# Partition sums of the first modulation as one-column products on TensorE, with the last two pieces of sc1 multiplied there too

## What is computed

```python
mod = (silu(c) @ w_ada + b_ada)            # 1024 x 6144 weights
sh1, sc1, g1, sh2, sc2, g2 = jnp.split(mod, 6, axis=-1)
h = rms_norm(x, norm1_g) * (1.0 + sc1) + sh1
proj = h @ w_in                            # q, k, v and pool part u
x = x + g1 * (concat[attention(q, k, v), pooling(u)] @ w_o)
h2 = rms_norm(x, norm2_g) * (1.0 + sc2) + sh2
x = x + g2 * (relu(h2 @ w_mlp_in) ** 2 @ w_mlp_out)
```

## Time and profile before

| what | us |
|---|---|
| median of 3 runs | 965.35 |
| lowest and highest of them | 964.99, 967.53 |
| the profiled execution, its own time | 964.76 |
| its span, first to last instruction | 963.0 |
| PE busy in the span | 923.1 (96%) |
| DVE busy | 656.4 (68%) |
| ACT busy | 491.4 (51%) |
| POOL busy | 348.6 (36%) |

### The profile page before, as it was taken

The page is one execution under the profiler, slowest core; times in us unless marked ns, Lnnn a source line. Parts: engine busy times, 40 slices in busy tenths (PEclk is TensorE's granted clock), DMA queues, the critical chain, the costliest instruction groups (busy, mean ns, idle before and its releaser), DMA issues.

```text
span 963.0 us, 12639 instructions
## 1 busy us (share of the span) xinstructions
PE 923.1 (96%) x4411; PEld 762.8 (79%) x4411; DVE 656.4 (68%) x1000; ACT 491.4 (51%) x874; POOL 348.6 (36%) x342
## 2 busy tenths in 40 slices
PE   1899999998999999999999999999999999999998
PEld 1787788886778888788888788888888888888887
DVE  6976887878554587665566544535687666789896
ACT  1756677778465564645544455454343544333331
POOL 8041211116232443988788877851000000000000
PEclk9999999999999999999999999999999999999999
DMA  9852432214222240765456534548998837997772
GB/s 357 323 170 74 131 110 88 80 54 155 87 88 88 88 153 22 232 203 177 164 168 203 176 132 134 173 143 274 331 354 292 280 98 235 312 323 233 237 248 105
DMA packets 92271, 175.54 MB, mean 182 GB/s; under 512 B 9320, under 2 KB 26288, under 8 KB 92208
## 3 DMA queue, kind: packets, MB, share of 16 engines
q1 hardware_dynamic: 92096, 174.70, 54.0%
q10 hardware_dynamic: 112, 0.04, 0.0%
HBM read 136.95 MB, written 37.75 MB: 181 GB/s over the span
## 4 chain that ended last, share of the span: by engine, by line
PE 84%; DVE 7%; ACT 5%; issue 2%; DMA 1%; SPq 1%; POOL 0%; DVEq 0%; ACTq 0%
PE psum L1965 26%; PE psum L1967 26%; PE psum L1966 25%; PE psum L1961 3%; DMA slots<-in_w_ada 1%; ACT probs L777 1%; PE psum L2041 1%; ACT qT L796 1%; DVE squares L1162 1%; PE psum L2091 1%; PE psum L2022 1%; PE psum L2020 1%; PE psum L2019 1%; ACT probs L785 1%; PE psum L2064 1%
## 5 line engine op out<-in xcount | busy, mean ns | idle before, releaser
L1072 ACT CAST down_operands<-down_raw 128x1024 fp32r<-128x1024 f32 x96 | 100.9, 1054 | 152.5 <-PE psum L1967 57.6
L1965 PE MATMUL psum<-down_operands 128*128 128x512 f32 x448 | 174.3, 389 | 0.0
L1966 PE MATMUL psum<-down_operands 128*128 128x512 f32 x448 | 174.3, 389 | 0.0
L1967 PE MATMUL psum<-down_operands 128*128 128x512 f32 x448 | 174.3, 389 | 0.0
L1701 DVE TENSOR_TENSOR down_operands<-down_raw,down_operands 128x1024 fp32r<-128x1024 f32 x93 | 112.4, 1220 | 16.3 <-ACT down_operands L1072 15.4
L1965 PE MATMUL psum<-h2T,w_operands 128*128 128x512 f32 x272 | 107.4, 395 | 1.9 <-DVE act_quads_a L1645 1.3
L1967 PE MATMUL psum<-h2T,w_operands 128*128 128x512 f32 x272 | 106.0, 390 | 0.0
L1966 PE MATMUL psum<-h2T,w_operands 128*128 128x512 f32 x272 | 105.9, 389 | 0.0
L1917 POOL TENSOR_TENSOR w_operands<-raw,w_operands 128x512 fp32r<-128x512 f32 x56 | 83.1, 1485 | 42.2 <-ACT w_operands L1024 42.2
L1966 PEld LDWEIGHTS psum<-down_operands 128*128 128x128 f32 x448 | 84.1, 188 | 17.6
L1965 PEld LDWEIGHTS psum<-down_operands 128*128 128x128 f32 x448 | 84.1, 188 | 17.5
(11 more groups left out here) (249 smaller groups left out, 1965.5 us busy)
## 6 DMA issues: line engine op xcount, KB each, us to landing
down_raw<-in_w_mlp_out SPq DMA_DIRECT2D x160, 256.0 KB, 4.5
down_raw<-act_scratch SPq DMA_DIRECT2D x112, 256.0 KB, 3.4
raw<-in_w_ada SPq DMA_DIRECT2D x32, 512.0 KB, 4.5
raw<-in_w_mlp_in SPq DMA_DIRECT2D x32, 512.0 KB, 4.8
act_scratch<-act_quads_a SPq DMA_DIRECT2D x64, 256.0 KB, 2.3
act_scratch<-act_quads_b SPq DMA_DIRECT2D x48, 256.0 KB, 3.5
slots<-in_w_ada SPq DMA_DIRECT2D x8, 512.0 KB, 10.5
xh<-in_x SPq DMA_DIRECT2D x8, 512.0 KB, 5.8
```

The source lines that it names most:

```text
L1072: nc.scalar.copy(o[:, 0, :, :], r[:, 0:2, :]).then_inc(op2_hi, 1)
L1965: mm(o, wh, ah, start=first, stop=False, skip_group_check=adds)
L1966: mm(o, wh, al, start=False, stop=False, skip_group_check=adds)
L1967: return mm(o, wl, ah, start=False, stop=last, skip_group_check=adds)
```

## The change

Transposes and free-axis sums are replaced with products of one column. For each 128x128 block n of an accumulator, `column_sum` makes the block the stationary operand and a column of ones the moving one, so that the sum over partitions lands as one PSUM column (bank `at + n // 4`, column `n % 4`). For the last two pieces of sc1 (numbers 6 and 7) DVE does nothing more: the piece itself is the stationary operand, and silu[:, k] the moving column, so that multiplication and sum over partitions happen in one product, accumulated in the same PSUM columns. On PE the sh1 sums are 8 such products; for sc1 there are 8 on piece 6, 8 on `acc_sc` and 8 on piece 7, in that order, and after piece 7's fourth and eighth the two halves are signalled. `keep_clock(6, 2)` goes away. On DVE the copy of `cols` moves to just behind the last sh1 piece, the finish of sh1 becomes one addition of 128x8, and `scale_1` becomes two small instructions. The buffer of piece 6 is free once its products are done (`sc1_used`), that of piece 7 once the second half is signalled. SP, ACT and POOL keep their orders.

```diff
@@ -231,6 +231,7 @@
         EARLY_USE = EARLY // WIDE + 1
         MLP_USE = EARLY_USE + (len(stream) - 4 - EARLY) // RING
         WO_POOL, WO_DVE = (0, 5, 6), (1, 2, 3, 4, 7)
+        SC1_DVE = KD - 2
         JOB_LOADS = (4, 4, 4, 3, 4, 4, 1, 0)
         adaln_jobs = ("sh2", "sc2", "g1", "g2")
         mod_of = {"sh1": SH1, "sc1": SC1, "g1": G1, "sh2": SH2, "sc2": SC2, "g2": G2}
@@ -266,6 +267,7 @@
         g1_in = sem("g1_in")
         mod_turned = sem("mod_turned")
         sc1_turned = sem("sc1_turned")
+        sc1_used = sem("sc1_used")
         mod_taken = sem("mod_taken")
 
         a1_ready = sem("a1_ready")
@@ -472,7 +474,12 @@
             kind, k = stream[before]
             if kind in ("sh1", "sc1"):
 
-                eng.wait_ge(mod_summed, k + 1 + (KD if kind == "sc1" else 0) + (kind == "sc1" and k == KD - 1))
+                if kind == "sc1" and k == SC1_DVE:
+                    eng.wait_ge(sc1_used, 1)
+                elif kind == "sc1" and k == KD - 1:
+                    eng.wait_ge(sc1_turned, 2)
+                else:
+                    eng.wait_ge(mod_summed, k + 1 + (KD if kind == "sc1" else 0))
             elif kind in adaln_jobs:
                 eng.wait_ge(job_summed, KD * adaln_jobs.index(kind) + k + 1)
             elif kind == "x":
@@ -1188,40 +1195,35 @@
                 own_d.wait()
                 v.tensor_scalar(a1_, a3, -1.0, float(np.pi / 2), ALU.mult, ALU.add).then_inc(angles_ready, 1)
 
-            for n in range(2 * KD):
+            for n in range(KD + SC1_DVE):
                 if n >= 1:
                     dve.wait_ge(mod_summed, n)
                 if n < KD:
                     add_piece(acc[:, :], ("sh1", n), n, mod_summed)
-                elif n < 2 * KD - 1:
+                else:
                     add_piece(acc_sc, ("sc1", n - KD), n - KD, mod_summed)
-                else:
-                    a = landed(dve, ("sc1", KD - 1))
-                    for h in range(2):
-                        cut = slice(512 * h, 512 * h + 512)
-                        v.scalar_tensor_tensor(out=acc_sc[:, cut], in0=a[:, cut], scalar=silu[:, KD - 1:KD],
-                                               in1=acc_sc[:, cut], op0=ALU.mult, op1=ALU.add).then_inc(mod_summed, 1)
                 if n == 4:
                     dve.wait_ge(rows_in, 16 * 4)
                     v.tensor_copy(rows[64:72, :], posi[64:72, :]).then_inc(posf_ready, 1)
-                if n == KD + 2:
+                if n == KD - 1:
 
                     dve.wait_ge(rows_turned, 1)
                     v.tensor_copy(cols[:, :], psum[:, 4, 0:72]).then_inc(cols_ready, 1)
-                if n == 2 * KD - 4:
+                if n == KD + 4:
 
                     dve.wait_ge(cols_ready, 1)
                     dve.wait_ge(mod_turned, 1)
-                    v.tensor_reduce(b1, banks(0).rearrange("p (k n) -> p k n", n=P), AX_X, ALU.add).then_inc(mod_taken, 1)
+                    v.tensor_tensor(b1.rearrange("p (h k) -> p h k", h=2), psum[:, 0:2, 0:4],
+                                    cols[:, 8 * SH1:8 * SH1 + 8].rearrange("p (h k) -> p h k", h=2),
+                                    ALU.add).then_inc(mod_taken, 1)
+
+            def scale_1(h):
+
+                c4 = slice(4 * h, 4 * h + 4)
+                if h == 0:
                     dve.wait_ge(mod_taken, 1)
-                    own_d.step(v.tensor_tensor(b1, b1, cols[:, 8 * SH1:8 * SH1 + 8], ALU.add))
-            def scale_1(h):
-
-                c4 = slice(4 * h, 4 * h + 4)
                 dve.wait_ge(sc1_turned, h + 1)
-                own_d.step(v.tensor_reduce(a1[:, c4], bank(2 + h).rearrange("p (k n) -> p k n", n=P), AX_X, ALU.add))
-                own_d.wait()
-                own_d.step(v.tensor_tensor(a1[:, c4], a1[:, c4],
+                own_d.step(v.tensor_tensor(a1[:, c4], psum[:, 2 + h, 0:4],
                                            cols[:, 8 * SC1 + 4 * h:8 * SC1 + 4 * h + 4], ALU.add))
                 own_d.wait()
                 v.scalar_tensor_tensor(out=a1[:, c4], in0=a1[:, c4], scalar=1.0, in1=cols[:, 48 + 4 * h:52 + 4 * h],
@@ -2098,17 +2100,32 @@
             pe.wait_ge(posf_ready, 1)
             tr(psum[:, 4, 0:72], rows[0:72, :], 72).then_inc(rows_turned, 1)
 
+            def column_sum(at, n, a, by, first, last):
+
+                to = psum[:, at + n // 4, n % 4:n % 4 + 1]
+                return mm(to, a[:, n * P:(n + 1) * P], by, start=first and n % 4 == 0, stop=last, skip_group_check=True)
+
             pe.wait_ge(mod_summed, KD)
-            turn_sums(banks(0), acc).then_inc(mod_turned, 1)
+            for n in range(KD):
+                ins = column_sum(0, n, acc, ones[:, 0:1], True, True)
+            ins.then_inc(mod_turned, 1)
             pe.wait_ge(mod_summed, 2 * KD - 5)
             keep_clock(8, 2)
             turn_x(0)
             pe.wait_ge(cols_ready, 1)
             turn_x(1)
-            keep_clock(6, 2)
+            a = landed(pe, ("sc1", SC1_DVE))
+            for n in range(KD):
+                ins = column_sum(2, n, a, silu[:, SC1_DVE:SC1_DVE + 1], True, False)
+            ins.then_inc(sc1_used, 1)
+            pe.wait_ge(mod_summed, KD + SC1_DVE)
+            for n in range(KD):
+                column_sum(2, n, acc_sc, ones[:, 0:1], False, False)
+            a = landed(pe, ("sc1", KD - 1))
             for h in range(2):
-                pe.wait_ge(mod_summed, 2 * KD + h)
-                turn_sums(bank(2 + h), acc_sc[:, 512 * h:512 * h + 512]).then_inc(sc1_turned, 1)
+                for n in range(4 * h, 4 * h + 4):
+                    ins = column_sum(2, n, a, silu[:, KD - 1:KD], False, True)
+                ins.then_inc(sc1_turned, 1)
             pe.wait_ge(mod_taken, 1)
             keep_clock(14, 0)
 
```

More of the change, by code:

```diff
@@ L1206, in _ @@
                     v.tensor_copy(rows[64:72, :], posi[64:72, :]).then_inc(posf_ready, 1)
-                if n == KD + 2:
+                if n == KD - 1:
                     dve.wait_ge(rows_turned, 1)
                     v.tensor_copy(cols[:, :], psum[:, 4, 0:72]).then_inc(cols_ready, 1)
-                if n == 2 * KD - 4:
+                if n == KD + 4:
                     dve.wait_ge(cols_ready, 1)
                     dve.wait_ge(mod_turned, 1)
-                    v.tensor_reduce(b1, banks(0).rearrange("p (k n) -> p k n", n=P), AX_X, ALU.add).then_inc(mod_taken, 1)
-                    dve.wait_ge(mod_taken, 1)
-                    own_d.step(v.tensor_tensor(b1, b1, cols[:, 8 * SH1:8 * SH1 + 8], ALU.add))
+                    v.tensor_tensor(b1.rearrange("p (h k) -> p h k", h=2), psum[:, 0:2, 0:4],
+                                    cols[:, 8 * SH1:8 * SH1 + 8].rearrange("p (h k) -> p h k", h=2),
+                                    ALU.add).then_inc(mod_taken, 1)
             def scale_1(h):
                 c4 = slice(4 * h, 4 * h + 4)
+                if h == 0:
+                    dve.wait_ge(mod_taken, 1)
                 dve.wait_ge(sc1_turned, h + 1)
-                own_d.step(v.tensor_reduce(a1[:, c4], bank(2 + h).rearrange("p (k n) -> p k n", n=P), AX_X, ALU.add))
-                own_d.wait()
-                own_d.step(v.tensor_tensor(a1[:, c4], a1[:, c4],
+                own_d.step(v.tensor_tensor(a1[:, c4], psum[:, 2 + h, 0:4],
                                            cols[:, 8 * SC1 + 4 * h:8 * SC1 + 4 * h + 4], ALU.add))
```

## The result

| | before | after |
|---|---|---|
| median of 20 runs, us | 965.41 | 969.38 |
| lowest and highest | 964.77, 967.53 | 965.51, 975.00 |
| profiled execution | 964.76 | 973.25 |
| its span | 963.0 | 971.5 |

The changed kernel takes 1.0043 times the time of before, 95% interval 1.0030 to 1.0056: **4.2 us slower**. The forecast was 965.8 with a range to 969.2. What is new beside the median is the spread: before, 20 executions lie within 2.8 us, after within 9.5. The lowest of after is 0.7 above the lowest of before, close to the forecast sum.

A forecast was written before the change was run, and what follows sets the result against it. DVE was taken to bound the kernel from 30.47 to 49 us, with PE setting the end behind. A signal 1.90 us later less 1.45 us spared gave +0.45 on 965.35: 965.8 us, range 963.6 to 969.2.

The forecast's parts named there:

- What bounds the kernel: DVE bounds from the first sc1 half's signal (30.47 us) until 49 us; behind that PE sets the end.
- A record at 0.112 us: Each one-column weight load and product on PE costs 0.112 us, as with 128 columns; 0.21 at the slow clock.
- the handover: From the fortieth load to DVE's start: 0.11, a product of 0.17 (0.275 less 0.107 of streaming), and 0.04; 0.32 us.
- Sum +0.45: First sc1 signal +1.90 us later, DVE spared 1.45 us of free-axis sums behind it; net +0.45 us, chance 0.62.
- The step that failed: PE reaches the sc1 columns at 27.68 us, behind the x transposes, and runs 40 records at 0.112 us each.
- a rival at 0.18: PE's clock falls early in the column products, 26 of 40 records slow: +3.7 us, 969.1 us; chance 0.18.
- With all records slow: All column records at the slow clock, with 28 slow filler records behind: w_in at 44.0 us, +6.5, 971.8 us.
- The small edits: sh1 products, the filler behind the columns and later SP loads, each covered by waiting time or slack, cost nothing.
- None of this counts: DVE's savings ahead of the signal (pieces 6 and 7, sh1 sum, cols copy) add nothing, as PE is late next.
- `keep_clock(14, 0)` level, at no cost: Its 28 records behind the last column end near 36.2 us, when project_u(0) can start; no cost.
- PE's slack: 48 w_in products from 35.76 us would end at 46.8, but the last begins at 48.56; some 1.8 us.
- SP and the buffers: The load waiting for piece 7's buffer goes out at 33.3 us, not 30.4; even 2.9 us later it is in time.

The follow-up runs named there:

- a_root: Changed kernel with GpSimd's roots for x tiles 0 and 1 moved ahead of the last pooling band (early roots): 968.12 us, ratio 1.0021.
- b_root: Kernel before with GpSimd's roots for x moved ahead of the last pooling band: 964.55 us, ratio 0.9990.
- probe_columns: Kernel before with 48 one-column products of the identity matrix put between keep_clock(14, 0) and project_u(0): 979.93 us in one execution.
- a_again: Changed kernel run once more, unaltered, for a second profile: 970.73 us.
- a_clock6: Changed kernel with keep_clock(6, 2) put back ahead of the sc1 column products: 972.25 us, ratio 1.0054.
- sc1_alone: Kernel before with only the sc1 part of the change, sh1 left as before: 967.76 us, ratio 1.0032.
- a_firm: a_root with keep_clock(10, 2) moved ahead of the x transposes and keep_clock(6, 2) right ahead of the sc1 columns: 966.55 us, ratio 1.0007.
- probe_transposes: Kernel before with 96 transposes of the identity matrix put between keep_clock(14, 0) and project_u(0): 971.91 us in one execution.
- sums_root: Kernel before with both sums over partitions as one-column products, all pieces on DVE, keep_clock(6, 2) kept, GpSimd's roots early: 963.74 us, ratio 0.9977.
- sums_only: Kernel before with both sums over partitions as one-column products, all pieces on DVE, keep_clock(6, 2) kept, roots not moved: 966.86 us, ratio 1.0005.
- a_held: a_root with four full products behind the 8 columns on piece 6 and again behind the 8 on the accumulator: 968.47 us, ratio 1.0024.
- sums_early: sums_root with keep_clock(10, 2) straight behind the sh1 columns and keep_clock(8, 2) in place of 6: 962.50 us, ratio 0.9965.

## Why the prediction was wrong, point by point

- **What bounds the kernel.** Right for before. Everything behind the stage shifts by what is lost up to there (8.5 us at 75 us and at the end). But the bound did not stay with DVE: in after it is PE's order, through the transposes, the columns and the filler.
- **A record at 0.112 us.** Right, at the fast level: 0.112 in both probes and in a_root. The floor of about 25 ns that the prediction quotes from the Trainium skill (TensorE: Matmul & The Clock Gate, "Back-to-back issue gap") does not come up in any run here, where each product brings a new weight load and the spacing is the same for 1 column as for 128. At the slow level 0.21, as bounded. One term of the handover has no row: the 0.107 of streaming that was taken off the last record. One-column records of a fast stream last 0.250, not 0.17; the signal came 0.11 sooner than forecast all the same.
- **Sum +0.45.** Right in the one profiled execution in which its condition held. a_root: signal at 32.26 for 32.37, DVE's stretch from the signal to `lo_wu` 1.95 us for 3.40, so 1.45 spared as worked out, end +0.36 (+0.57 over b_root's, which has early roots too).
- **The step that failed** is the one that gave this the chance of 0.62: that PE reaches the columns at 27.68 with the clock fast, and that it stays so. Both halves were wrong. In each of the six profiles whose columns began fast and had no full product among them (probe_columns, a_again, a_clock6, sc1_alone, a_root, a_firm) the clock fell 3.0 to 5.4 us after the first, and the columns last 5.4 us. In after it was not even up when they began, at 30.46 and not at 27.68. I had this as a rival at 0.18 and priced it at 969.1, next to the 969.38 measured, from a count of slow records that was a guess, so that the two agree is luck. With all records slow I had 971.8 and w_in at 44.0; after's profile has 973.25 and 46.35, chiefly since the columns also began 2.8 us late. The range went only to the middle of that rival, and ended 0.2 short. No row of before could show the stretch, but "no row shows such a stretch" was a reason to give it more, not less.
- **The small edits.** I listed what DVE was spared and asked who waits for it, but not who else uses the time: GpSimd, whose 0.72 us become 1.77 when a piece on SBUF stands in the place of the sh1 sum. Whether "None of this counts" failed by this is not shown, as the starts of x's scaling overlap. What did fail is the 27.68 as a fixed time. It rested on one trace, and in the nine profiles with GpSimd's old order ACT begins to scale x anywhere between 24.4 and 26.9 us.
- **`keep_clock(14, 0)` level, at no cost.** Right in a_root (4.83 us, hidden), wrong wherever it is slow from its first record: 5.7 to 5.95 us. PE's slack was forecast at 1.8 and is 2.0 in probe_transposes. The slip is in the working: it holds the end of 48 products (46.8) against the start of the last (48.56); start against start, 48.56 − (35.76 + 47 x 0.23), is 2.0. With it the first score product comes out: after 10.6 − 2.0 = 8.6, measured 8.6; a_firm 3.9 − 2.0 = 1.9, measured 1.9.
- **SP and the buffers.** No share: in after ACT and DVE wait for no w_in piece that was moved.

How the 4.2 us divide: by the ratios 2.1 go away with early roots (1.0043 to 1.0021, a_root), of which b_root gains 1.0 without the change, and 1.4 more with the filler moved ahead (to 1.0007, a_firm), rounded and with intervals of about 1 us each way. I read the 1.4 as the level at which the columns begin, but no slow execution of a_root was profiled to show it, and the moved filler was not tried on the kernel before. Over b_root a_firm is still 1.0017, or 1.6 us, and not the 0.45 of the forecast: its profile has the fall and a filler at the slow level. I did not run the change with the filler behind the columns taken out, so how much of the PE path that filler alone carries is arithmetic, not shown.

## What to carry to other kernels

One-column products on PE cost as much as ones of 128 columns where each has its own weight load, 0.112 us per record at the fast clock. In this kernel a stretch of them lost that clock 3.0 to 5.4 us after it began and slowed what stood behind it, while 16 records (1.8 us) in sums_root and sums_only did not. So use them for a few blocks, not as the main work of a stage. When an engine is relieved of work, look for what ran beside it: the same GpSimd instruction took 0.72 us beside a DVE sum on PSUM and 1.77 beside pieces on two SBUF tensors. Give an edit that helps both kernels to both before you divide a loss by it. A wide spread between executions of one program can come from the clock, so take a second profile before trusting one.

## What was not expected of the hardware

- The clock falls under one-column products though PE is busy without a pause (2.00 of 2.00 us in probe_columns) and its weight loads come every 0.112 us; 96 transposes at the same rate keep it for 10.5 us.
- It falls elsewhere too, in some executions and not in others: behind the same pauses of 1.11 and 0.72 us ahead of w_o it fell in a_held and not in before, and cost 1.2 us.
- A record of one column lasts 250 ns in a stream at the fast level (352 at the slow), hardly less than one of 128 columns (275), at the same spacing.
- Beside DVE's multiply-add of 128x1024 on SBUF a GpSimd copy of 128x1 takes 1.2 us (without it 0.18), and the power of 128x2 takes 1.8 (beside the sum on PSUM 0.72, in a_root at 18.46 us 1.09).
- After a fall PE made full products at the slow level for 3.4 us (a_root, sums_early) to 5.7 us (a_firm) before it was fast again, and the fall in sums_early came when the columns were over and full products ran.
- The granted clock reads 1.00 over stretches at the start that durations show to be slow (421 ns against 275), and 0.50 only after a first rise and fall.
